# Triangular inverse of a gated delta net: 16x16 base blocks solved on GpSimd through DRAM tables in place of 8x8 blocks selected on TensorE

## The chip, the cores and the metric

The kernel runs on one core of one Trainium2 chip. The metric is device time in microseconds, as the median of several runs of the whole program. The program is one launch; all data is float32.

## What is computed

The reference is a trunk of two residual layers: a bidirectional gated delta net, a mixture of experts, multi-head latent attention, and the mixture again. Only the delta net is touched by the change. Its core, cut from the reference, for one direction:

```python
k_beta = k * beta[..., None]
a = jnp.where(strict, jnp.einsum('nbhcd,nbhsd->nbhcs', k_beta, k) * decay, 0.0)
t_inv = lax.linalg.triangular_solve(a + eye, eye, left_side=True, lower=True, unit_diagonal=True)
u = jnp.einsum('nbhcs,nbhsd->nbhcd', t_inv, v * beta[..., None])
w = jnp.einsum('nbhcs,nbhsd->nbhcd', t_inv, k_beta * jnp.exp(g)[..., None])
# then a recurrence over chunks with state S; the same on the flipped sequence; the sum is
# normalised, gated with silu(z) and multiplied by w_out
```

There are 512 tokens, model width 1024, 8 key heads of 128, and 16 value heads of 128, two for each key head. What matters here is t_inv, the inverse of a unit triangular matrix, for each chunk, each value head and each of the two directions.

## The kernel before

The function delta_net writes one block of instructions for each engine. It works in chunks of P = 128 tokens, so a sequence has TT = 4 tiles, and loops over the NK = 8 key heads. Head 0 is projected and prepared ahead of the loop; body(0, FIRST) and body(7, LAST) are written out, and a hardware loop runs body(i, MAIN) for heads 1 to 6, the middle heads. All orders are written out by hand; engines meet through semaphores.

Body i does the inverse and the recurrence of head i and, in the same time, the projections of head i + 1 and the output projection of head i - 1.

**The inverse.** mask_scores leaves A (the masked scores, for two value heads h and four tiles). compact() on VectorE picks the 8x8 diagonal blocks out of A into A8 and forms factors. Seven B steps then solve all the 8x8 blocks of both directions: in each, TensorE multiplies R8 with constant selection matrices (line 572), and VectorE multiplies and subtracts (lines 1154, 1156). VectorE spreads the blocks to 128x128 tiles of TU (line 1164), and four groups of sixteen transposes (line 582) with ScalarE copies give the turned form. Then levels l = 3 to 6 double the block each time: X = A T (make_x, line 592), masked by VectorE (line 1145), Y and V (make_y, make_v, lines 598 and 604), and updates of T and U by VectorE (line 1150). ScalarE copies the older blocks to W ahead of each level (line 803).

**What stands between.** TensorE carries a list of fillers. In FIRST and MAIN these are the 32 projection matmuls of head i + 1 (project, line 455; bank 0 or 1): eight ahead of the B steps, the rest between the steps and in the levels. In LAST they are the output projections y of head 6. VectorE's between(slot) does the convolution taps, the scans of the gate spans (line 1006), and the silu products of head i + 1 in the same manner.

**The rest of the body.** Four recurrence steps, with the gate projection z (make_z, line 541) in them; then prepare (sixteen transposes, line 510), the output projections y0 to y7 of head i - 1 (line 500) with turn_kq behind y3 (it waits for the normalised kq: squares on ScalarE, key sums on VectorE, rsqrt on GpSimd at lines 165 and 167, then normalise) and scores (line 528) behind y5; and turn_o (line 663), eight transposes.

**GpSimd** per head: the taps copies (line 909), four products qkd (line 923) once the scores are masked, two span additions (line 899), and the small rsqrt steps. **SP** issues, in a loop over n: load_w(n + 1), load_z(n), load_spans(n + 1); behind the loop the rows of the norm, and eight small transfers of the layer norm gains and biases (line 398 to tapr, semaphore cols_in; line 399 to gain_cols), then the first expert weights. In LAST, TensorE waits for cols_in behind its first three fillers.

A record in the trace is half a float32 matmul: each 128x512 matmul shows as two records, and so does each 128x128 one; a transpose shows as one.

Of the kernel before, what the change touches and what calls it, by code (L numbers as in the profile page):

```python
# [26 lines left out]
LEVELS, BASE = 7, 3  # L27
# [13 lines left out]
C_BLK = C_ROW + 8 * P  # L41
C_UNIT = C_BLK + P
C_SIDE = C_UNIT + 8
C_SEAT = C_SIDE + 16
# [6 lines left out]
def constants():  # L51
# [17 lines left out]
    for k in range(8):  # L69
        c[:, C_ROW + k * P:C_ROW + (k + 1) * P] = r == q // 8 * 8 + k  # L70
    c[:, C_BLK:C_BLK + P] = r // 8 == q // 8
    for at, value in ((C_HALF, -0.5), (C_EPS_K, 4.0 * RMS_EPS), (C_EPS_O, DH * RMS_EPS), (C_EPS_LN, LN_EPS), (C_ZERO, 0.0)):
        c[:, at:at + 8] = value
    eight = np.arange(8)[None, :]
    c[:, C_UNIT:C_UNIT + 8] = r % 8 == eight
    c[:, C_SIDE:C_SIDE + 8] = eight > r % 8
    c[:, C_SIDE + 8:C_SIDE + 16] = eight < r % 8
# [48 lines left out]
OUTPUT = [(f"y{n}", n % 2) for n in range(8)]  # L126
PREPARE_LATE = [("kT", 2), ("qT", 3), ("KK", 2), ("KQ", 3)]


def dn_uses(with_next, with_last):  # L130

    names = list(PROJECT if with_next else OUTPUT)
    names += [(f"B{m}", 4 + m % 2) for m in range(7)] + [("G0", 6), ("G1", 7), ("G2", 2), ("G3", 3)]
# [4 lines left out]
    names += [("z0", 0), ("z1", 1)]  # L138
# [5 lines left out]
    if with_next:  # L144
        names += PREPARE + OUTPUT * with_last + PREPARE_LATE + TURN_O
    else:
        names += TURN_O + [(f"end{n}", n % 2) for n in range(8)]
# [22 lines left out]
def delta_net(nc, t, dram):  # L170
# [10 lines left out]
    with ExitStack() as ctx:  # L181
# [25 lines left out]
        TU = ring[3].rearrange("p (w d h t n) -> p w d h t n", w=2, d=2, h=2, t=TT)  # L207
        bc = sb("bc", [P, 2, 2 * TT])
        A8 = sb("A8", [P, 2 * TT, 8])
        side = sb("side", [P, 2, 8, 2 * TT])  # L210
        co = sb("co", [P, 2, 8, 2 * TT])
        R8 = sb("R8", [P, 2, 2 * TT, 8])
        part8 = sb("part8", [P, 2, 2 * TT, 8])
# [13 lines left out]
        tmp = TU[:, 1, 1, 1].rearrange("p t n -> p (t n)").rearrange("p (f t g) -> p f t g", f=4, t=TT)  # L227
# [13 lines left out]
        beta_row_ready = sem("beta_row_ready")  # L241
        rows_in, R_ready, B_read, block_ready, turned_ready = (sem(n) for n in ("rows_in", "R_ready", "B_read", "block_ready", "turned_ready"))
# [18 lines left out]
        earlier = {0: 2, 1: 2, 2: 2, 3: 1, 4: 4, 5: 4, 6: 1, 7: 0}  # L261
        base = {b: n + FIRST_HEAD.per.get(b, 0) for b, n in earlier.items()}

        def read_of(name, i):
# [14 lines left out]
            if name[0] == "B":  # L279
                return B_read, i * 7 + int(name[1]) + 1  # L280
            if name[0] == "G":
                return turned_ready, i * 4 + int(name[1]) + 1
# [27 lines left out]
        def merged(which, h, l, tt=None):  # L310

            b = 1 << l
            whole = TU[:, which, 0, h]
            first, tiles = (0, TT) if tt is None else (tt, 1)
            return bass.AP(whole.tensor, whole.offset + first * P, [list(whole.ap[0]), [2 * b, tiles * P // (2 * b)], [2 * TT * P + b, 2], [1, b]])

        def row_factors(m):

            return bass.AP(co, co[:, 0, 7 - m].offset, [list(co[:, 0, 0].ap[0]), [8 + 16 * m, 2], [1, 2 * TT], [0, 8]])

        def spread(d, h):

            one = R8[:, d, h * TT]
            return bass.AP(R8, one.offset, [list(one.ap[0]), [8, TT], [0, 16], [1, 8]])

# [12 lines left out]
        def _(sp):  # L338
# [31 lines left out]

            load_w(0, False)
# [7 lines left out]
            load_z(0, False)  # L379
            load_w(1, True)  # L380
            load_rows_of_norm(sp, t, dram, 0)
# [3 lines left out]
            load_spans(1)  # L385
            sp.wait_ge(zeroed, 1)
# [30 lines left out]
        def _(pe):  # L417
# [41 lines left out]
            def log_sums():  # L459
# [9 lines left out]
                mm.then_inc(full[6], 1)  # L469

# [60 lines left out]
            def body(i, uses, with_next):  # L531
# [13 lines left out]
                if with_next:  # L545
                    for ct in range(4):
                        for a in range(KD):
                            fill.append((project, (uses, i, i + 1, ct, (a, a + 1))))
                else:
                    for n in range(8):  # L550
                        for h in range(2):
                            fill.append((project_out, (uses, "y", i, i - 1, n, h)))

                def filler(n=1):
                    for _ in range(n):
                        if fill:
                            f, a = fill.pop(0)
                            f(*a)

                filler(8 if with_next else 3)  # L560
# [4 lines left out]

                pe.wait_ge(rows_in, 16)
                for m in range(7):
                    pe.wait_ge(R_ready, i * 8 + m + 1)
                    bank = begin(uses, f"B{m}", i)
                    for d in range(2):  # L570
                        k = m if d else 7 - m
                        mm = pe.matmul(bank[:, d * 64:(d + 1) * 64], c[:, C_ROW + k * P:C_ROW + (k + 1) * P], R8[:, d].rearrange("p g j -> p (g j)"), start=True, stop=True)
                    done(mm, uses, f"B{m}")
                    filler(2 if with_next and m < 6 else 1)
                filler()
                if not with_next:
                    pe.wait_ge(weighted, 1)
                for g in range(4):
# [2168 lines left out]
```

## Time and profile before

| | |
|---|---|
| median of 3 runs | 1528.35 us (1528.23 to 1530.12) |
| span of the profiled execution | 1527.5 us |
| TensorE busy | 1457.1 us (95%), 8226 matmul records |
| TensorE weight loads | 901.5 us (59%) |
| VectorE busy | 887.9 us (58%) |
| ScalarE busy | 373.7 us (24%) |
| GpSimd busy | 169.8 us (11%) |
| mean granted TensorE clock | 0.985 |
| DMA, mean over the span | 141 GB/s |

The table counts busy time over the whole program; the delta net ends at about 850 us. TensorE's busy time contains the overlap of pipelined matmuls, so the length of a group is best read from the start of one group to the start of the next. The granted clock is a share of full speed, 1.00 or 0.50.

### The profile page before, as it was taken

The numbers are of one execution on the slowest core, as the hardware profiler recorded it, in microseconds if no ns is written. First come the engines' busy times: TensorE is split into PE (matmuls) and PEld (weight loads), VectorE is DVE, ScalarE is ACT, GpSimd is POOL, SyncE is SP. The second block draws the span as 40 slices with busy tenths as digits, with TensorE's granted clock in tenths as the row PEclk, the third lists the DMA queues.
The fourth block names the chain that finished last, engine by engine and source line by source line (L and its number), as shares of the span: only waits on it lengthen the run. The fifth ranks groups of instructions, "written<-read, shape, count | busy, mean of one in ns | idle before, by whom it ended". The sixth has DMA issues, their size and how long they took to land. (4 is left out here: it accounts for less than half of the span.)

```text
span 1527.5 us, 22499 instructions
## 1 busy us (share of the span) xinstructions
PE 1457.1 (95%) x8226; PEld 901.5 (59%) x8226; DVE 887.9 (58%) x1800; ACT 373.7 (24%) x831; POOL 169.8 (11%) x196
## 2 busy tenths in 40 slices
PE   8799999999999999999999889999999999899896
PEld 5478686685776866857769543334654454543332
DVE  2775776766857767668575545317435454734227
ACT  3223222222222222222212222110333222122210
POOL 1200203002002030020010120003100000120011
PEclk9899999999999999999999899999999999899998
DMA  7760312102121121020250469997021115489983
GB/s 223 232 210 26 99 29 83 40 15 87 39 67 52 29 82 38 17 82 0 58 191 28 151 245 399 399 362 233 0 75 44 38 39 213 158 305 400 400 327 126
DMA packets 126625, 215.50 MB, mean 141 GB/s; under 512 B 13809, under 2 KB 61233, under 8 KB 126561
## 3 DMA queue, kind: packets, MB, share of 16 engines
q1 hardware_dynamic: 112096, 169.46, 32.0%
q10 hardware_dynamic: 9536, 27.27, 4.8%
q0 software_dynamic: 4928, 17.89, 3.2%
q8 instruction: 43, 0.70, 0.2%
q14 instruction: 22, 0.17, 0.0%
HBM read 182.95 MB, written 31.65 MB: 140 GB/s over the span
## 5 line engine op out<-in xcount | busy, mean ns | idle before, releaser
L455 PE MATMUL bank<-xT,wgu 128*128 128x512 f32 x448 | 210.8, 601 | 0.0
L1798 PE MATMUL bank<-wgu,moe_xgT 128*32 128x512 f32 x1536 | 169.8, 594 | 4.4 <-issue 4.0
L500 PE MATMUL bank<-wd,oT 128*128 128x512 f32 x256 | 118.1, 604 | 2.2 <-ACT oT L849 1.3
L541 PE MATMUL bank<-wd,xT 128*128 128x256 f32 x512 | 119.8, 380 | 0.0
L455 PEld LDWEIGHTS bank<-xT,wgu 128*128 128x128 f32 x448 | 78.5, 192 | 64.4 <-issue 63.7
L1798 PEld LDWEIGHTS bank<-wgu,moe_xgT 128*32 128x32 f32 x1536 | 50.4, 110 | 105.8 <-issue 95.1
L1029 DVE SCALAR_TENSOR_TENSOR wgu<-bank,taps,wgu 128x510 f32<-128x510 f32 (+1 forms) x128 | 95.3, 745 | 12.2 <-ACT wgu L744 8.1
L541 PEld LDWEIGHTS bank<-wd,xT 128*128 128x128 f32 x512 | 95.1, 191 | 11.4
L1821 PE MATMUL bank<-wd,moe_hidT 128*32 128x512 f32 x768 | 87.1, 593 | 7.2 <-issue 4.1
L2065 DVE TENSOR_TENSOR moe_hid<-moe_silu,bank 128x256 f32<-128x256 f32 x24 | 10.1, 422 | 128.7 <-ACT moe_silu L1908 128.7
L1150 DVE TENSOR_TENSOR wgu<-wgu,bank 128x512 f32<-128x512 f32 x112 | 73.9, 683 | 9.0 <-PE bank L604 3.4
L500 PEld LDWEIGHTS bank<-wd,oT 128*128 128x128 f32 x256 | 46.9, 194 | 49.1 <-issue 49.0
L604 PE MATMUL bank<-late,wd 128*128 128x128 f32 x512 | 67.2, 277 | 0.3
L592 PEld LDWEIGHTS bank<-wgu,wd 128*128 128x128 f32 x512 | 62.0, 192 | 8.4 <-issue 7.2
L2633 DVE TENSOR_REDUCE mla_mx<-bank 128x1 f32<-128x512 f32 x32 | 22.0, 686 | 74.2 <-PE bank L2400 74.2
L1122 DVE TENSOR_TENSOR res<-res,bank 128x512 f32<-128x512 f32 x64 | 43.9, 685 | 35.3 <-PE bank L500 34.9
L592 PE MATMUL bank<-wgu,wd 128*128 128x128 f32 x512 | 64.2, 278 | 0.0
L604 PEld LDWEIGHTS bank<-late,wd 128*128 128x128 f32 x512 | 61.6, 192 | 1.7 <-DVE wd L1145 1.6
L1821 PEld LDWEIGHTS bank<-wd,moe_hidT 128*32 128x32 f32 x768 | 26.5, 110 | 60.5 <-issue 60.2
L831 ACT ACTIVATE vs<-bank,gb 128x128 f32<-128x128 f32 x96 | 30.5, 375 | 108.8 <-PE bank L641 108.8
L598 PEld LDWEIGHTS bank<-wd,late 128*128 128x128 f32 x384 | 48.6, 192 | 11.5 <-issue 11.5
L1145 DVE TENSOR_TENSOR wd<-bank,masks 128x512 f32<-128x512 f32 x64 | 44.1, 690 | 18.5 <-PE bank L592 17.4
(344 smaller groups left out, 2390.5 us busy)
## 6 DMA issues: line engine op xcount, KB each, us to landing
wgu<-moe_w_gate SPq DMA_DIRECT2D x32, 1024.0 KB, 14.2
wgu<-moe_w_up SPq DMA_DIRECT2D x32, 1024.0 KB, 15.5
wd<-moe_w_down SPq DMA_DIRECT2D x32, 1024.0 KB, 15.9
wgu<-dn_w_in SPq DMA_DIRECT2D x32, 512.0 KB, 4.0
slots_x<-gains SPq DMA_DIRECT2D x1, 9984.0 KB, 37.9
wd<-dn_w_in SPq DMA_DIRECT2D x8, 1024.0 KB, 5.5
wd<-dn_w_out ACTq DMA_DIRECT2D x16, 512.0 KB, 3.9
xT<-slots_x ACTq DMA_DIRECT2D x16, 512.0 KB, 8.5
```

Source lines behind the costliest of these rows:

```text
L455: mm = pe.matmul(bank[:], wqkv[:, ct, k], xT[:, k], start=k == 0, stop=k == KD - 1)
L500: mm = pe.matmul(ps[uses.at[f"{name}{n}"][0]][:], oT[:, h, tt], wo[:, h, half * 512:(half + 1) * 512], start=h == 0, stop=h == 1)
L541: mm = pe.matmul(bank[:, (n % 2) * 256:(n % 2) * 256 + 256], xT[:, k, tt * P:(tt + 1) * P], wz[:, k], start=k == 0, stop=k == KD - 1)
L592: mm = pe.matmul(bank[:, tt * P:(tt + 1) * P], A[:, h, tt], merged(0, h, l, tt), start=True, stop=True)
L598: mm = pe.matmul(bank[:, tt * P:(tt + 1) * P], W[:, h, tt], X[:, h, tt], start=True, stop=True)
L604: mm = pe.matmul(bank[:, tt * P:(tt + 1) * P], X[:, h, tt], W[:, h, tt], start=True, stop=True)
L1029: ins = nc.vector.scalar_tensor_tensor(out=conv[:, ct, lo:hi], in0=bank[:, lo + d:hi + d], scalar=w[:, j:j + 1], in1=conv[:, ct, lo:hi], o ...
L1122: nc.vector.tensor_tensor(y, y, bank[:], ALU.add).then_inc(y_ready, 1)
L1145: nc.vector.tensor_tensor(X[:, h], bank[:].rearrange("p (t n) -> p t n", t=TT), m, ALU.mult).then_inc(xm_ready, 1)
L1150: nc.vector.tensor_tensor(merged(which, h, l), merged(which, h, l), change, ALU.subtract).then_inc(U_ready if which else T_ready, 1)
L1798: mm = pe.matmul(ps[2][seats].rearrange("p (a f) -> p a f", a=2), xgT[:, j % ROW_BUFS, k, seats], wgu[:, e % RING, :, k], start=k == 0, st ...
L1821: mm = pe.matmul(ps[4 + half][seats], hidT[:, f, seats], wd[:, e % RING, f, half * 512:(half + 1) * 512], start=f == 0, stop=f == 1)
```

## The change

The base of the doubling goes from 8x8 to 16x16 blocks, so level 3 is gone, and the blocks are found in another way. compact(), the seven B steps, the G transposes, the spreading and their constants are removed.

SP gets solve_blocks(n): it writes A to a DRAM table A_rows (two transfers of 256 KB), waits for them, reads the diagonal blocks of 16 rows of 64 bytes into raw_blk so that each partition holds one block (four transfers, 128 partitions of 256 elements), waits for T_solved, writes the solved blocks in both forms to the diagonals of the DRAM table T_rows (two transfers of 2048 pieces of 64 bytes; off the diagonal the table was zeroed at the start), waits for T_kept, and loads the full tiles of TU back (four transfers of 512 KB, in 512-byte pieces, semaphores T_in[0] and T_in[1]).

GpSimd gets solve(i), behind qkd and ahead of the span additions of the next head: a copy of the head's betas, a scaled mask, four products S, the diagonal, 28 dependent small operations (14 columns, each a product and an addition) and two products for the two forms.

The order changes. TensorE's body begins with all 32 projection matmuls of head i + 1; then comes make_x of level 4, which waits for T_in. The fillers in the levels are now y0 to y3 of head i - 1 (all in bank 0), and only y4 to y7 remain behind the recurrence, with turn_kq behind y4 and scores behind y6. VectorE does the scans, the taps of three tiles and two silus ahead of the levels. In LAST, TensorE waits for cols_in first, then does y0 to y3 and all of z, and y4 to y7 stand in the recurrence steps. SP's order at the start and in the loop changes around solve_blocks: the large zero fill of slots_x and the rows of the norm now stand behind solve_blocks(0), and the norm rows and cols transfers at the end stand behind solve_blocks(7).

The core of the diff:

```diff
-LEVELS, BASE = 7, 3
+LEVELS, BASE = 7, 4
...
+            def solve_blocks(n):
+
+                for h in range(2):
+                    sp.wait_ge(at_ready, n * 2 + h + 1)
+                    sp.dma_start(tiles_of(t["A_rows"])[:, 4 * h:4 * h + 4], A[:, h]).then_inc(A_kept, 16)
+                sp.wait_ge(A_kept, (n + 1) * 32)
+                for h in range(2):
+                    for d in range(2):
+                        sp.dma_start(raw_blk[h * 64 + d * 32:h * 64 + d * 32 + 32], diagonal(t["A_rows"], 4 * h, 32)).then_inc(blocks_in, 16)
+                sp.wait_ge(T_solved, n + 1)
+                if head_zero(n):
+                    sp.wait_ge(padded, 16)
+                for f in range(2):
+                    sp.dma_start(diagonal(t["T_rows"][f], 0, P), T_blk[:, f]).then_inc(T_kept, 16)
+                sp.wait_ge(T_kept, (n + 1) * 32)
+                for h in range(2):
+                    for f in range(2):
+                        sp.dma_start(forms[:, f, h].rearrange("p d t n -> p (d t) n"), tiles_of(t["T_rows"][f])[:, 8 * h:8 * h + 8]).then_inc(T_in[h], 16)
...
             with sp.Fori(1, NK - 1) as n:
                 load_w(n + 1, True)
                 load_z(n, True)
                 load_spans(n + 1)
+                solve_blocks(n)
             load_z(NK - 1, True)
+            solve_blocks(NK - 1)
             sp.wait_ge(zero_filled, 32)
             load_rows_of_norm(sp, t, dram, 1)
...
                 if with_next:
                     for ct in range(4):
-                        for a in range(KD):
-                            fill.append((project, (uses, i, i + 1, ct, (a, a + 1))))
...
+                        project(uses, i, i + 1, ct)
+                if uses is not FIRST:
+                    for n in range(4 if with_next else 8):
+                        fill.append((uses, "y", i, i - 1, n))
...
                 if not with_next:
                     pe.wait_ge(cols_in, 64)
                     pe.wait_ge(*last_read(2, i))
                     pe.matmul(ps[2][:, 0:4 * KD], cols[:], ident[0:4 * KD, 0:4 * KD], start=True, stop=True).then_inc(cols_turned, 1)
...
+                    filler(4)
+                    pe.wait_ge(z_in, (i + 1) * 16)
+                    for n in range(TT):
+                        make_z(n)
                     pe.wait_ge(weighted, 1)
...
                 def make_x(l, h):
                     if l == BASE:
-                        pe.wait_ge(turned_ready, i * 4 + 2 * h + 2)
+                        pe.wait_ge(T_in[h], (i + 1) * 32)
...
+            def solve(i):
...
+                step(nc.gpsimd.tensor_tensor(scaled[:], upper, over_rows, ALU.mult))
+                pool.wait_ge(blocks_in, (i + 1) * 64)
+                for part in range(4):
+                    some = slice(32 * part, 32 * (part + 1))
+                    raw = raw_blk[some].rearrange("p r c -> p c r") if part % 2 else raw_blk[some]
+                    step(nc.gpsimd.tensor_tensor(S[some], raw, scaled[some], ALU.mult))
+                step(nc.gpsimd.tensor_tensor(S[:].rearrange("p r c -> p (r c)")[:, 0:BLK * BLK:BLK + 1], ones[:, 0:BLK], ones[:, 0:BLK], ALU.mult))
+                for k in range(BLK - 2, 0, -1):
+                    n = BLK - 1 - k
+                    part = prod[:, 0:k * n].rearrange("p (r c) -> p r c", r=k)
+                    step(nc.gpsimd.tensor_tensor(part, S[:, 0:k, k:k + 1].to_broadcast([P, k, n]), S[:, k:k + 1, k + 1:].to_broadcast([P, k, n]), ALU.mult))
+                    step(nc.gpsimd.tensor_tensor(S[:, 0:k, k + 1:], S[:, 0:k, k + 1:], part, ALU.add))
+                nc.gpsimd.tensor_tensor(T_blk[:, 1], S[:], over_cols, ALU.mult)
+                nc.gpsimd.tensor_tensor(T_blk[:, 0], S[:].rearrange("p r c -> p c r"), over_rows, ALU.mult).then_inc(T_solved, 1)
```

## Rows read from the trace of the kernel before

**Rows 1.** Windows: busy us of each engine in one middle head, clock, DMA.

```profile
360.10:453.20 93.10, 92.88 (x491) 68.96 (x490) 63.51 (x126) 24.55 (x55) 11.54 (x10) 1.00 0.14 40
```

**Rows 2.** Timeline of TensorE, same head: start us, us, line, operation, records.

```profile
345.03 1.91 PE L510 MATMUL bank<-masks,wgu 128*128 128x128 f32 x16
346.77 7.03 PE L500 MATMUL bank<-wd,oT 128*128 128x512 f32 x16
...
357.95 1.95 PE L528 MATMUL bank<-kqT 128*128 128x128 f32 x16
359.74 3.60 PE L500 MATMUL bank<-wd,oT 128*128 128x512 f32 x8
...
364.12 7.13 PE L455 MATMUL bank<-xT,wgu 128*128 128x512 f32 x16
371.09 0.55 PE L572 MATMUL bank<-R,masks 128*128 128x64 f32 x4
371.48 1.94 PE L455 MATMUL bank<-xT,wgu 128*128 128x512 f32 x4
...
386.23 2.29 PE L582 MATMUL bank<-masks,wgu 128*128 128x128 f32 x16
388.35 2.07 PE L592 MATMUL bank<-wgu,wd 128*128 128x128 f32 x16
390.26 1.88 PE L455 MATMUL bank<-xT,wgu 128*128 128x512 f32 x4
391.98 1.05 PE L598 MATMUL bank<-wd,late 128*128 128x128 f32 x8
...
395.55 1.88 PE L455 MATMUL bank<-xT,wgu 128*128 128x512 f32 x4
```

**Rows 3.** Timeline of VectorE in the same head.

```profile
359.13 1.29 DVE L1070 TENSOR_TENSOR wd<-wgu,bank 128x512 f32<-128x512 f32 x2 [0.21 <-PE bank L528]
...
391.91 1.22 DVE L1006 TENSOR_TENSOR_SCAN wgu<-wgu 128x512 f32<-128x512 f32 x1
```

**Rows 4.** Timeline of GpSimd in it; last, a group over the program (mean ns).

```profile
348.08 0.20 POOL L165 TENSOR_TENSOR kq_rs<-kq_ss,masks 128x8 f32<-128x8 f32 x1 [4.54 <-DVE kq_ss L1053]
348.36 1.64 POOL L167 TENSOR_TENSOR kq_rs<-kq_rs,masks 128x8 f32<-128x8 f32 x1
...
361.76 5.95 POOL L923 TENSOR_TENSOR wd<-wgu 128x512 f32<-128x512 f32 x4 [3.26 <-DVE wgu L1074]
...
L909 POOL COPY taps<-tap_all 128x5 f32 x12 | 7.5, 650 | 0.0
```

**Rows 5.** DMA issues by line: KB each, median us from issue to landing.

```profile
wgu<-dn_w_in SPq DMA_DIRECT2D x32, 512.0 KB, 4.0
...
wd<-dn_w_in SPq DMA_DIRECT2D x8, 1024.0 KB, 5.5
...
gate_rows<-late POOLq DMA_DIRECT2D x1, 64.0 KB, 2.1
```

**Rows 6.** DMA packets in the stretch 761.5 to 762.0.

```profile
DMA packets 1119, 0.03 MB, mean 58 GB/s; under 512 B 1100, under 2 KB 1116, under 8 KB 1119
```

**Rows 7.** The third qkd alone (min/median/max ns), and VectorE beside it.

```profile
L923 POOL TENSOR_TENSOR wd<-wgu x1: 2254/2254/2254, 364.2 to 364.2; 128x512 f32<-128x512 f32 x1
...
363.98 1.37 DVE L1083 TENSOR_TENSOR wd<-wd,masks 128x1024 f32<-128x1024 f32 x1
```

**Rows 8.** Windows ahead of the first head; the clock is the third number from the end.

```profile
56.00:59.20 3.20, 0.00 (x0) 0.00 (x0) 1.13 (x3) 0.49 (x1) 2.29 (x5) 0.50 1.07 377
59.20:65.20 6.00, 5.96 (x25) 5.49 (x26) 2.15 (x4) 1.17 (x2) 0.00 (x0) 0.50 0.85 251
```

**Rows 9.** Timeline of SP's queue ahead of the last head, first and last of ten.

```profile
754.53 0.57 SPq L1315 DMA_DIRECT2D gains<-ln_g  x1
...
759.25 0.69 SPq L398 DMA_DIRECT2D tapr<-ln_b  x1
```

More of the change, by code:

```diff
@@ L312, in merged @@
             b = 1 << l
-            whole = TU[:, which, 0, h]
+            one, other = (TU[which][dd][:, h, 0] for dd in range(2))
             first, tiles = (0, TT) if tt is None else (tt, 1)
[L315 to L324, printed above, removed]
+            return bass.AP(one.tensor, one.offset + first * P, [list(one.ap[0]), [2 * b, tiles * P // (2 * b)], [other.offset - one.offset + b, 2], [1, b]])
         def z_pair(a, n):
@@ L469, in log_sums @@
                 mm.then_inc(full[6], 1)
+                for tt in range(TT):
+                    mm = pe.transpose(ps[7][0:2 * NV, tt * P:(tt + 1) * P], gt[:, BETA, tt], ident)
+                mm.then_inc(full[7], 1)
             def turn_taps():
@@ L556, in filler @@
                         if fill:
-                            f, a = fill.pop(0)
-                            f(*a)
-                filler(8 if with_next else 3)
+                            one = fill.pop(0)
+                            for h in range(2):
+                                project_out(*one, h)
                 if not with_next:
@@ L609, in body @@
                     make_x(l, 1)
-                    filler(2 if with_next else 1)
+                    if with_next and l > BASE:
+                        filler()
                     for h in range(2):
@@ L616, in body @@
                         make_v(l, h)
-                    filler(2 if with_next else 1)
-                filler(99)
+                    if with_next and l < LEVELS - 1:
+                        filler()
                 pe.wait_ge(z_in, (i + 1) * 16)
@@ L668, in body @@
                     prepare(uses, i, i + 1)
-                    for n in range(8):
+                    for n in range(4, 8):
+                        if n == 5:
+                            turn_kq(uses, i, i + 1)
                         if uses is MAIN:
@@ L923, in body @@
                         nc.gpsimd.tensor_tensor(qkd[:, 2 * d + h], dec[:, h], kqm[:, d], ALU.mult).then_inc(qkd_ready, 1)
+                solve(i)
                 if with_next:
@@ new lines, in body @@
+                    jobs["window"] = [lambda n=n: span(i + 1, n // 2, n % 2) for n in range(4)]
+                    for ct in range(3):
+                        jobs["window"] += taps_apart(ct)
+                        if ct:
+                            jobs["window"].append(lambda ct=ct: silu(i + 1, ct - 1))
+                    for slot, job in enumerate(taps_apart(3)):
+                        jobs[slot] = [job]
+                    jobs[4] = [lambda: silu(i + 1, 2)]
+                    jobs[8] = [lambda: silu(i + 1, 3)]
```

245 lines of the change are left out of this document (106 added, 139 removed).

## The prediction

> **What bounds the kernel now.** I read the busy times of one whole head first, then TensorE in order of time, then the other engines and the queues inside the same head. In a middle head TensorE is busy 92.88 of 93.10 us at the full clock [rows 1], and in order of time its groups follow each other without a gap [rows 2]. So the delta-net heads are bound by TensorE's own work: what is removed from it comes off the time, as long as nothing it then waits for arrives later than the work that remains. The whole question is therefore how long the new road from the score matrix A to the 16x16 blocks takes, and how much TensorE work stands beside it.
>
> **What is removed from TensorE, a head.** A B step goes from 371.09 to 371.48, 0.39 us; seven are 2.7. The sixteen G transposes go from 386.23 to 388.35, 2.1. Level 3 is its X, 388.35 to 390.26, 1.9, and its Y and V, 391.98 to 395.55, 3.6 [rows 2]. Sum 10.3 us of the head, 82 us in eight. VectorE's compact(), its fourteen small operations and its level 3 go too, but it waits for TensorE today, so I price them at nothing.
>
> **The cover.** Let K be the end of the KK scores, 358.85 (half of the scores that start at 357.95 and are followed at 359.74). After the change TensorE has, behind K: KQ 0.9, y7 1.7, turn_o 1.0, and all 32 projection matmuls. Sixteen records of 512 columns take 364.12 to 371.09, 0.43 us each [rows 2]; 64 are 27.9. X of level 4 is reached at K+31.5 and X of the second value head at K+32.4. That last one needs T_in[1], the last transfer.
>
> **The new chain, from K.**
> - VectorE's masks and kqm end and GpSimd starts qkd at 361.76, K+2.9 [rows 3, 4]. A itself is ready at K+1.6; writing it (two issues, 2.1 us as for gate_rows) and reading the 64-byte rows back (four issues of 0.4, 2.1 us and 2048 packets) ends about K+9 to K+12 [rows 5, 6], beside GpSimd's own work below, so GpSimd decides.
> - qkd: three of four take 1.23 us each ((5.95 - 2.25)/3), so 4.9 [rows 4]. The four scans of VectorE, 1.22 each [rows 3], are now first in its window, right on top. The third qkd took 2.25 us in place of 1.23, while VectorE ran a product of two SBUF tensors from 363.98 [rows 7]. The scan reads two SBUF tensors as well. Bounds 0 and 4.9; I take 4.0, since the one row that overlaps lost about all of the overlap. Then beta and scaled, 1.1. K+12.9.
> - The solve: a 4 to 8 element operation costs 0.20 and the next dependent one starts 0.28 after it [rows 4]; from there to 512 elements the slope is 2.04 ns an element. Four S products of 256 elements, 3.2; the diagonal 0.3; 28 dependent steps, 28 x 0.28 + 1120 elements x 2.04 ns = 10.1; two T_blk 1.4. Sum 15.0, and 0.7 for the silu products of VectorE in the same window. K+28.6.
> - T to DRAM: 4096 packets of 64 bytes. Issue 0.8, fixed part 2.1 [rows 5]. Small packets (8 bytes nearly all) went at 1119 in 0.5 us on the 16 DMA engines, 7 ns each on one engine [rows 6]; the 512-byte ones of a projection weight at (4.0 - 2.1) us for 1024, 30 ns [rows 5]. So 1.8 to 7.7 us; no row has small writes to DRAM. I take 4.7, the middle. Together 7.6. K+36.2.
> - T back: 2.1 MB in four transfers. The z weight gives 1.05 MB in 5.5 - 2.1 us, 308 GB/s [rows 5]; 6.8 + 2.1 = 8.9. K+45.1.
> So TensorE idles 45.1 - 32.4 = 12.7 us a head, against 10.3 saved.
>
> The SBUF page of the Trainium skill ("SBUF — State Buffer", Who interferes with whom) says that a VectorE instruction with two SBUF inputs contends with a GpSimd instruction that reads SBUF, and that the loser blocks for the whole instruction; the trace agrees (2.25 against 1.23 us), and without that rule the sum would be 4.7 us shorter a head. The DMA page ("DMA: Bandwidth & Descriptors", Specifications) says that below 512 bytes a DMA reads, modifies and writes, and it speaks against the 64-byte stores; no row here shows it, and it gives no time of its own.
>
> **What else changes.** (a) TensorE's turn_kq waits for kq. Today four output projections (346.77 on) cover that chain; now only y4 does. Key sums end at 348.08, the power ends at 350.0, one VectorE product of 0.65 makes it 350.7; TensorE is there at 346.77 + 1.72 = 348.5 [rows 2, 4]. 2.3 us idle in each middle head. (b) After the idle 56.0 to 59.2 the granted clock was 0.50 for 6.0 us of work [rows 8], which is the level of 1.2 GHz in place of 2.4; it lost 3.0 us. A gap of 12.7 us should cost the same: 3.0 a head. (c) The levels have half the filler, but VectorE and ScalarE have one level and all small steps less beside them; nothing, and 1 for the first head, which has no filler. (d) spans, z weights and the next projection weights stand in SP's queue around solve_blocks. The spans and z are issued before it, the weights of n+2 after T_kept, a whole level stage before they are needed; nothing. (e) The zero fill moves behind head 0's solve and has 40 us of slack; nothing. (f) four BETA transposes and beta's rows at the start: 1 us.
>
> **The last head.** SP issues the norm rows and the cols transfers only behind solve_blocks(7), which waits for T_kept. But in the last body TensorE waits for cols_in before its first filler. So the y and z work that is meant to cover the solve starts only when cols is in. There the scans are missing: T_kept at 45.1 - 8.9 - 4.7 = K+31.5. Four T_in issues 1.6, then norm and cols issues, 754.53 to 759.94 = 5.4 [rows 9], K+38.5; T_in and norm rows are 3.1 MB in the same rings, 10.2 us from K+31.9, so cols lands at K+44.2. TensorE waits from K+3.6: 40.6 us. Less 10.3, plus 3.0 clock, plus 2 for recurrence steps in which y (1.7 us) stands in for z (16 records of 256 columns, 3.5): +35.3.
>
> **Sum.** Six middle heads: -10.3 + 12.7 + 2.3 + 3.0 = +7.7 each, +46. First head: its cover lacks y7 and turn_o (2.7), but its kq wait is there today: -10.3 + 15.4 + 3.0 = +8.1, with 1 for missing fillers +9. Last +35, start +1. Together +91 on a span of 1527.5: 1618.5, and 0.85 us lie between this span and the median: 1619. With no lock and 7 ns packets the chain is 37.5, the idle 5.1: +0.1 x 6 + 2 + 32 + 1 = +36, 1564. With 30 ns packets and the lock in full, 3.9 more in each of eight heads: 1650.
>
> The Trainium skill ("GPSIMD Engine Reference", Performance pitfalls) has reads with a step of over 8 bytes 50% dearer; no row here shows it, and it would add 1.2 us a head.
>
> **Rivals.** (1) The road is cheap: small packets near 7 ns, no lock that matters. 1564, still slower, because the last head's wait and the kq wait stay. For it: the 7 ns row. Against: those are loads. 0.18. (2) The cover holds and it is faster: the chain is under 32.4 us from K, 12.7 less than my sum, so that the 10.3 come off whole. Place: T_in[1] in the middle heads; it decides from K+32.4. Middle -8.0 x 6, first -10, last 35 - 13 = +22, start +1: -35, 1493. For it: each fixed part of 2.1 us may overlap with its issue and GpSimd's real spacing may be under its recorded spans. Against: GpSimd's steps alone end at K+24 without any lock, and two round trips of 2.1 us and 2.1 MB follow. 0.13. (3) GpSimd's small strided operations in the loop cost more: the taps copy of 5 elements took 0.65 us there [rows 4], 0.45 more than the step I price; 28 x 0.45 = 12.6 in eight heads, +101: 1720. Against: the rsqrt add, just as small, took 0.20. 0.14. (4) The change does not do what it says, the solve not being on the road at all: excluded by make_x's wait for T_in.
>
> **How the numbers follow.** Forecast as summed 0.55 (its own range 1564 to 1650), rivals 0.18, 0.13, 0.14. Range 1540 to 1700: it leaves out rival 2 and about half of rival 3. About 0.2% is what a measurement can tell from no change; only a mix of rival 1 and 2 lands there. Faster 0.13, same 0.02, slower 0.85.
>
> **What would show it.** Right: TensorE idle before line make_x at level 4 of some 13 us in each middle head, released by the DMA of T_rows; granted clock 0.5 behind it; an idle stretch of about 40 us in the last head ahead of the cols matmul; idle of 2 us ahead of the kq transposes; the third and fourth qkd or the scans stretched. Wrong: T_in landing before the projections end, dependent GpSimd steps spaced far from 0.28 us, T_rows writes landing in under 5 or over 11 us, or cols_in before the solve is written.

## The result and the profile of the changed kernel

The changed kernel takes 1593.12 us as the median of four runs (1592.22 to 1599.55), against 1528.66 us for the kernel before in the same session. The ratio is 1.0427, 95% interval 1.0406 to 1.0447: slower by 4.3%. The forecast was 1619 us with a range of 1540 to 1700, so its sign and its range held and its middle was 26 us too high. The profiled execution spans 1591.1 us, 63.6 more than that of before, at a mean granted clock of 0.942 (0.985 before).

The busy times on the page of the changed kernel, then a group of section 5 (busy us, mean ns of one | idle ahead of them and what ended it):

```profile
PE 1402.6 (88%) x7494; PEld 846.8 (53%) x7494; DVE 796.8 (50%) x1569; ACT 346.5 (22%) x767; POOL 296.0 (19%) x497
...
L595 PE MATMUL bank<-wgu,wd 128*128 128x128 f32 x384 | 62.1, 323 | 62.6 <-DMA wgu<-T_rows 62.6
```

TensorE has 54.5 us less busy time and still ends 63.6 us later: it stands idle. The waits of TensorE in the delta net's heads (us in total, times, longest) say for whom:

```profile
PE bank L595 <- DMA wgu<-T_rows: 62.6, 14, 10.1
PE bank L581 <- DMA tapr<-ln_b: 38.9, 1, 38.9
PE bank L538 <- DVE kq L1108: 19.2, 7, 4.2
```

L595 is make_x at level 4, which waits for the solved tiles; L581 is the cols matmul of the last head; L538 is turn_kq. Here is one middle head in order of time on TensorE. It is the part that answers to [rows 2]; K, the end of the KK scores, is 479.63.

```profile
474.21 1.25 PE L538 MATMUL bank<-masks,kq 128*128 128x128 f32 x8 [2.50 <-DVE kq L1108]
...
478.73 1.95 PE L547 MATMUL bank<-kqT 128*128 128x128 f32 x16
...
483.64 27.73 PE L471 MATMUL bank<-xT,wgu 128*128 128x512 f32 x64 [0.37 <-DVE res L1152]
518.01 2.07 PE L595 MATMUL bank<-wgu,wd 128*128 128x128 f32 x8 [6.64 <-DMA wgu<-T_rows]
521.62 2.07 PE L595 MATMUL bank<-wgu,wd 128*128 128x128 f32 x8 [1.54 <-DMA wgu<-T_rows]
523.49 1.92 PE L601 MATMUL bank<-wd,late 128*128 128x128 f32 x8
```

The projections end at K+31.7, and the two value heads of X start at K+38.4 and K+42.0. What happened on GpSimd in the same time (answering to [rows 4]):

```profile
482.54 7.70 POOL L957 TENSOR_TENSOR wd<-wgu 128x512 f32<-128x512 f32 x4 [7.46 <-DVE wgu L1120]
490.19 1.13 POOL L928 COPY beta_n<-beta_blk 128x16 f32 x1
491.40 0.73 POOL L934 TENSOR_TENSOR scaled<-masks,beta_n 128x256 f32<-128x256 f32 x1
492.29 3.35 POOL L939 TENSOR_TENSOR S<-raw_blk,scaled 32x256 f32<-32x256 f32 x4 [0.16 <-POOL scaled L934]
496.02 0.21 POOL L944 TENSOR_TENSOR prod<-S 128x14 f32<-128x14 f32 x1
...
505.97 0.62 POOL L946 TENSOR_TENSOR T_blk<-S,beta_n 128x256 f32<-128x256 f32 x1
506.55 0.84 POOL L947 TENSOR_TENSOR T_blk<-S,beta_n 128x256 f32<-128x256 f32 x1
```

On VectorE, the four scans lie on top of the qkd products, and SP issues the transfers (the length is that of the issues; answering to [rows 5]):

```profile
483.51 7.82 DVE L1052 TENSOR_TENSOR_SCAN wgu<-wgu 128x512 f32<-128x512 f32 x4
```

```profile
480.63 0.97 SPq L368 DMA_DIRECT2D A_rows<-wd  x2
483.85 1.92 SPq L372 DMA_DIRECT2D raw_blk<-A_rows  x4
507.41 1.38 SPq L377 DMA_DIRECT2D T_rows<-T_blk  x2
511.95 3.88 SPq L381 DMA_DIRECT2D wgu<-T_rows  x4
```

So the chain of one middle head, from K: qkd starts at 2.9 and takes 7.7; beta and scaled; S starts at 12.7; the 28 steps take 9.95 (496.02 to 505.97); both forms are done at 27.8; the store is issued and has landed, with its two issues, 4.5 us later (507.41 to 511.95); the loads bring the last tile at 42.0, 9.7 us on.

How fast the DMA engines moved the two kinds of pieces that the kernel stores, first A in pieces of 512 bytes, then T in pieces of 64 (the last two numbers are the DMA share and GB/s):

```profile
481.60:483.40 1.80, 1.67 (x10) 0.94 (x8) 1.80 (x4) 0.00 (x0) 0.86 (x1) 1.00 0.99 283
508.50:511.40 2.90, 2.88 (x7) 0.95 (x5) 0.66 (x1) 0.00 (x0) 1.78 (x2) 1.00 0.82 87
```

The granted clock behind the idle stretch (columns as in [rows 1]):

```profile
516.00:518.00 2.00, 0.00 (x0) 0.00 (x0) 0.00 (x0) 0.09 (x1) 0.00 (x0) 0.50 1.21 290
522.00:524.00 2.00, 2.00 (x11) 2.00 (x11) 0.20 (x1) 0.14 (x1) 0.00 (x0) 0.50 1.22 290
526.00:530.00 4.00, 4.00 (x25) 3.37 (x24) 2.95 (x6) 0.77 (x2) 0.00 (x0) 0.86 0.02 6
```

0.50 is the level of 1.2 GHz in place of 2.4: eight records of X take 2.07 us here, and sixteen took 2.07 before [rows 2].

The last head, on TensorE and on SP. Its cols matmul is reached right behind turn_o and waits 38.9 us; the issue it waits for is the last line, behind the store, the loads and the norm rows.

```profile
799.69 1.04 PE L670 MATMUL bank<-masks,late 128*128 128x128 f32 x8
839.62 0.63 PE L581 MATMUL bank<-masks,tapr 32*128 32x32 f32 x2 [38.89 <-DMA tapr<-ln_b]
840.18 9.29 PE L519 MATMUL bank<-wd,oT 128*128 128x512 f32 x16
```

```profile
821.12 1.34 SPq L377 DMA_DIRECT2D T_rows<-T_blk  x2
825.64 3.99 SPq L381 DMA_DIRECT2D wgu<-T_rows  x4
829.67 1.74 SPq L1331 DMA_DIRECT2D gains<-ln_g  x1
...
834.67 0.41 SPq L414 DMA_DIRECT2D tapr<-ln_b  x1
```

**Where the 63.6 us lie**, by the starts of the same TensorE work in both traces. From the scores of head 0 to turn_o behind head 0: 97.4 us before, 101.1 after, +3.7. Six middle heads, from turn_o to turn_o: 612.3 before, 637.4 after, +25.0 or 4.2 each. The last, from turn_o to the beta product behind the delta net (L680, now L687): 71.9 before, 102.6 after, +30.7. Everything behind that: 684.7 before, 688.8 after, +4.1. The start is 0.1 later.

A middle head adds up: -10.3 of removed work, +8.2 idle for the solved tiles, +2.5 for kq, +0.4 ahead of the projections (VectorE's addition of y), and the half clock: 0.9 on X of the first value head (2.07 against 1.16 at the full clock) and 2.6 from the second X on (the experiment e6 gives that), together +4.3.

### The profile page after: what moved, and what is told of

It reads as the page before. It is cut to its first block and busy times, and to the rows that moved or that the text cites. A ratio compares the mean times of both kernels' runs of the same rounds, so it can differ in the third digit from the quotient of the medians.

```text
span 1591.1 us, 21047 instructions
## 1 busy us (share of the span) xinstructions
PE 1402.6 (88%) x7494; PEld 846.8 (53%) x7494; DVE 796.8 (50%) x1569; ACT 346.5 (22%) x767; POOL 296.0 (19%) x497
## 5 line engine op out<-in xcount | busy, mean ns | idle before, releaser
L471 PE MATMUL bank<-xT,wgu 128*128 128x512 f32 x448 | 193.9, 593 | 1.9 <-DVE res L1152 1.9
L471 PEld LDWEIGHTS bank<-xT,wgu 128*128 128x128 f32 x448 | 84.6, 190 | 106.8 <-issue 103.7
L519 PE MATMUL bank<-wd,oT 128*128 128x512 f32 x256 | 123.1, 614 | 1.0 <-issue 1.0
L595 PE MATMUL bank<-wgu,wd 128*128 128x128 f32 x384 | 62.1, 323 | 62.6 <-DMA wgu<-T_rows 62.6
L595 PEld LDWEIGHTS bank<-wgu,wd 128*128 128x128 f32 x384 | 57.7, 232 | 76.1 <-issue 63.4
L1175 DVE TENSOR_TENSOR wd<-bank,masks 128x512 f32<-128x512 f32 x48 | 33.0, 689 | 102.1 <-PE bank L595 102.1
L2081 DVE TENSOR_TENSOR moe_hid<-moe_silu,bank 128x256 f32<-128x256 f32 x24 | 10.1, 421 | 131.8 <-ACT moe_silu L1924 131.8
L957 POOL TENSOR_TENSOR wd<-wgu 128x512 f32<-128x512 f32 x32 | 58.7, 1863 | 58.0 <-DVE wgu L1120 58.0
L813 ACT COPY late<-wgu 128x512 f32<-128x512 f32 x48 | 29.6, 618 | 165.2 <-DVE wgu L1180 101.8
L1180 DVE TENSOR_TENSOR wgu<-wgu,bank 128x512 f32<-128x512 f32 x80 | 54.5, 688 | 19.6 <-PE bank L607 13.3
L1463 POOL DMA_INDIRECT wgu<-slots_y,fetch x8 | 8.6, 1080 | 281.0 <-DMA slots_y<-moe_y_rows 268.6
L1052 DVE TENSOR_TENSOR_SCAN wgu<-wgu 128x512 f32<-128x512 f32 x32 | 58.6, 1886 | 4.6 <-DMA wgu<-gate_rows 4.6
## 6 DMA issues: line engine op xcount, KB each, us to landing
wd<-moe_w_down SPq DMA_DIRECT2D x32, 1024.0 KB, 15.7
```

Source lines behind the costliest of these rows:

```text
L471: mm = pe.matmul(bank[:], wqkv[:, ct, k], xT[:, k], start=k == 0, stop=k == KD - 1)
L519: mm = pe.matmul(ps[uses.at[f"{name}{n}"][0]][:], oT[:, h, tt], wo[:, h, half * 512:(half + 1) * 512], start=h == 0, stop=h == 1)
L595: mm = pe.matmul(bank[:, tt * P:(tt + 1) * P], A[:, h, tt], merged(0, h, l, tt), start=True, stop=True)
L957: nc.gpsimd.tensor_tensor(qkd[:, 2 * d + h], dec[:, h], kqm[:, d], ALU.mult).then_inc(qkd_ready, 1)
L1052: nc.vector.tensor_tensor_scan(row, row, mask, 0.0, ALU.add, ALU.mult).then_inc(span_ready, 1)
L1175: nc.vector.tensor_tensor(X[:, h], bank[:].rearrange("p (t n) -> p t n", t=TT), m, ALU.mult).then_inc(xm_ready, 1)
```

## The experiments

Each kernel is the changed one with one edit, unless said otherwise; the ratio is always to the kernel before, and the differences in us are between profiled spans, from 1591.1. The executions of one kernel lie 2.6 to 9.5 us apart, and the profiled one is the fastest of its kernel in e1, e5 and e6 and the slowest in e2 and e3, so a difference of spans is good to some 4 us; by the medians the savings are 23.7 (e1), 19.0 (e2), 33.1 (e3), 19.1 (e5), 8.5 (e6) and 19.6 (e7). What is read inside a head does not have this spread.

**e1: the gain columns ahead of the solve on SP.** This isolates the last head.

```diff
             load_z(NK - 1, True)
+            for j, (name, layer) in enumerate((("ln1_g", 0), ...)):    # cols and gain_cols
+                ...
             solve_blocks(NK - 1)
-            ...
```

> Change of the changed kernel: SP issues the cols and gain transfers of the last head ahead of solve_blocks(7) instead of behind it; all else is as in it. Theory (the last head pays for the order of SP's queue): the wait of 38.9 us for cols is gone, the y and z work runs while GpSimd solves, and TensorE then meets T_in after 25 us where it lands after some 38: about 28 us less, 1565 us, with a T_in wait of 10 to 12 us in the last head. Rival (that wait only stands in for the chain of the solve, which ends as late): 1590 or more.

Measured: median 1569.42, ratio 1.0254 (1.0214 to 1.0294), span 1563.3, 27.8 less. TensorE no longer stands ahead of the cols matmul; the work that was meant as cover now covers, and what is left is a wait for the tiles:

```profile
800.44 0.40 PE L581 MATMUL bank<-masks,tapr 32*128 32x32 f32 x2
802.23 7.11 PE L519 MATMUL bank<-wd,oT 128*128 128x512 f32 x16 [1.38 <-ACT oT L851]
```

The wait for the tiles in this head, next in line, is 8.4 us. From turn_o to the beta product the last head takes 76.2 us (799.48 to 875.71) in place of 102.6. So 26.4 of the 63.6 us are a matter of the order in one queue, not of the solve itself.

**e2: the four scans of VectorE behind the taps of three tiles,** so that they no longer run beside qkd.

```diff
-                    jobs["window"] = [lambda n=n: span(i + 1, n // 2, n % 2) for n in range(4)]
+                    jobs["window"] = []
                     for ct in range(3):
                         ...
+                    jobs["window"] += [lambda n=n: span(i + 1, n // 2, n % 2) for n in range(4)]
```

> Change of the changed kernel: VectorE's four scans stand behind the taps of the first three tiles instead of ahead of them, so that they run when GpSimd has ended its solve. Theory (GpSimd and two-SBUF-input VectorE work shut each other out): qkd goes from 7.7 to about 5.0 us a head, the scans from 2.2 to 1.2 us each, T_in lands 2.7 to 3.6 us earlier in seven heads, 1568 to 1574 us. Rival (GpSimd's products are as slow by themselves there): qkd stays at 7.7, 1593 us.

Measured: median 1574.08, ratio 1.0281 (1.0260 to 1.0301), span 1573.7, 17.4 less. The wait for T_rows is 42.5 us in place of 62.6. On GpSimd the four qkd products and the beta copy are short again:

```profile
473.43 4.96 POOL L957 TENSOR_TENSOR wd<-wgu 128x512 f32<-128x512 f32 x4 [7.46 <-DVE wgu L1120]
478.32 0.21 POOL L928 COPY beta_n<-beta_blk 128x16 f32 x1
```

4.96 against 7.70 and 0.21 against 1.13: the overlap with the scans costs the chain 3.7 us a head; here both forms of T are done at K+24.3 in place of K+27.8. The first middle head gains nothing, since its blocks land only at K+13.2. The scans pay as well: 7.82 us for four beside qkd, 1.22 each alone [rows 3]. The two groups together lasted 8.8 us (482.54 to 491.33), and one after the other they would last 9.8; running them side by side gains little. Single records of the changed kernel show how:

```profile
485.92 2.18 POOL L957 TENSOR_TENSOR wd<-wgu 128x512 f32<-128x512 f32 x1
486.96 2.22 DVE L1052 TENSOR_TENSOR_SCAN wgu<-wgu 128x512 f32<-128x512 f32 x1
```

The first product takes 1.28 us and the first scan 1.39; the other three of each take 2.2. They end in turn, product and scan, at 483.82, 484.90, 485.96, 487.04, 488.10, 489.18, 490.25 and 491.33, 1.1 us apart, and the beta copy of 16 elements ends together with the last scan (490.19 + 1.13 = 491.32). So a record of 2.2 us is one turn of waiting and one of work. This bears out for the scan too the rule that the prediction cites from the Trainium skill ("SBUF — State Buffer", Who interferes with whom), that the one that loses waits for the whole instruction of the other.

**e3: half of the columns of the solve.** Seven of the fourteen columns, so fourteen small operations, are left out; the inverse is then incomplete, so this time is only a dose of the chain's length.

```diff
-                for k in range(BLK - 2, 0, -1):
+                for k in range(BLK - 2, 7, -1):
```

> Change of the changed kernel: the solve does only the first 7 of its 14 column steps (the other seven are left out of the computation), 14 dependent small GpSimd operations less. Theory (GpSimd's string of small operations is on the road in every head): 14 x 0.35 = 5.0 us less wait in each of eight heads, 1553 us, somewhat less if the clock no longer falls. Rival (the transfers or the SP queue set the end): under 10 us less, 1585 or more.

Measured: median 1560.07, ratio 1.0182 (1.0151 to 1.0213), span 1559.6, 31.5 less. The wait for T_rows is 32.0 us, 30.6 less, or 4.4 in each of the seven heads that have it; that for cols is 34.1, 4.8 less, so cols does stand behind GpSimd's solve. Together 35.4 us of waits are gone and 31.5 came off the span; 1.7 of the difference lies behind the delta net. A middle head tells more: the second X starts 5.0 us earlier (K+37.0 in place of K+42.0 in the same head), and the head is only 3.6 us shorter (102.3 in place of 105.9). Behind the wait of 2.50 us for kq the two output projections take 5.2 to 5.3 us in all six middle heads, in place of 3.60; the granted clock is 0.64 from 559 to 563 us, behind such a wait. Doing half of the columns takes off half of what the change costs, so it would not pay for the change.

**e4 and e6: spare matmuls that keep TensorE at work in the gap,** to price the clock. They write a bank whose next real matmul starts it anew. e4 puts seven ahead of X of the first value head; e6 puts three more ahead of the second.

```diff
                 def make_x(l, h):
+                    if l == BASE and with_next:
+                        spare = begin(uses, f"X{l}{h}", i)
+                        for k in range((7, 3)[h]):
+                            pe.matmul(spare[:], xT[:, 0, 0:P], xT[:, k], start=True, stop=True)
                     if l == BASE:
```

> Change of the changed kernel: seven spare 512-column matmuls (6.0 us) into the bank of X stand ahead of the wait for T_in in every body but the last; their result is overwritten. Theory (the idle lets the granted clock fall and the work behind it pays): the clock stays at 1.00 around level 4, X, Y and V run at full rate, 3.3 us less in seven heads, 1570 us; the time of T_in's landing doesn't move. Rival (level 4 is slow because it waits for masks and copies): 1593 us or more.

Measured for e4: median 1596.46, ratio 1.0425 (1.0405 to 1.0445), span 1594.6, 3.5 more. The expectation failed. The first gap was filled and X of the first value head ran at the full clock (1.16 us), but a second idle stretch of 2.54 us follows it, and the clock fell there:

```profile
519.55 1.16 PE L599 MATMUL bank<-wgu,wd 128*128 128x128 f32 x8 [0.71 <-DMA wgu<-T_rows]
523.24 2.07 PE L599 MATMUL bank<-wgu,wd 128*128 128x128 f32 x8 [2.54 <-DMA wgu<-T_rows]
```

In one of the six middle heads the clock stayed at full speed behind the same idle of 2.53 us, and in four of them it fell later, behind the wait of 2.50 us for kq. So e4 did not separate anything, and e6 was made for it.

> Change of the changed kernel: spare matmuls ahead of both waits for T_in, seven ahead of X of the first value head and three between it and X of the second. The run with seven alone moved the idle behind the first X, where the clock then fell at 522 us all the same. Theory (the clock's fall costs 3.3 us a head): with no idle stretch of over 2 us left the clock stays at 1.00 through level 4, 18 to 23 us less than the changed kernel, 1572 us. Rival (it costs nothing that the wait would not cost): 1593 us.

Measured for e6: median 1584.63, ratio 1.0352 (1.0335 to 1.0369), span 1581.5, 9.6 less, half of what I expected. In the five later middle heads X and what follows run at the full clock (X takes 1.16 us); one of them:

```profile
515.71 1.16 PE L599 MATMUL bank<-wgu,wd 128*128 128x128 f32 x8 [0.62 <-DMA wgu<-T_rows]
...
519.32 1.16 PE L599 MATMUL bank<-wgu,wd 128*128 128x128 f32 x8
...
523.89 1.88 PE L519 MATMUL bank<-wd,oT 128*128 128x512 f32 x4
```

X of the second value head starts 42.89 us behind the start of the scores (476.43), just as in the changed kernel (478.73 to 521.62). From there to the first filler it is 4.57 us here, 7.18 there (521.62 to 528.80). So the half clock costs 2.6 us behind the second X; the 0.9 on the first X lies inside the wait for the second and gives nothing back. Over six heads that is 15.7, and in the span 9.6 came. In the first head level 4 ends at 111.94 against 112.35, so next to nothing came there. The trace shows where the rest went. In the first middle head a wait of 3.9 us is left, the clock falls behind it, and the six spare records take 4.4 us, so that the second X starts 2.2 us later than in the changed kernel. And in three of the six middle heads, that one among them, the clock falls later on, behind the wait for kq:

```profile
470.21 1.25 PE L538 MATMUL bank<-masks,kq 128*128 128x128 f32 x8 [2.50 <-DVE kq L1112]
471.30 5.30 PE L519 MATMUL bank<-wd,oT 128*128 128x512 f32 x8
```

5.2 to 5.3 us in place of 3.60; in the changed kernel this happens in the first middle head alone, and in part (4.66). From the scores of the first middle head to those of the last head e6 is 8.7 us shorter, which is most of the 9.6.

**e5: solve ahead of qkd on GpSimd.** VectorE's scans then meet the solve's wait for the blocks.

```diff
+                solve(i)
                 pool.wait_ge(dec_ready, i * 2 + 2)
                 pool.wait_ge(mask_ready, i * 2 + 2)
                 ...                                  # the four qkd products
-                solve(i)
```

> Change of the changed kernel: GpSimd does solve(i) ahead of its four qkd products instead of behind them. Theory (qkd stands on the road ahead of the solve, and the blocks land 2.7 us before GpSimd is free): T_in lands 2.7 us earlier in seven heads, nothing in the last one, 1574 us; the scans run beside an idle GpSimd at 1.2 us. Rival (the block reads land no earlier than GpSimd is free today): 1590 us or more.

Measured: median 1574.07, ratio 1.0278 (1.0261 to 1.0295), span 1568.9, 22.2 less; the wait for T_rows is 40.1. The four qkd products stood on the chain although the first to need them is the recurrence (L659). What is next late is the road of A: S now waits for raw_blk and starts at K+9.2, against K+12.7 in the changed kernel (K is 467.74 here).

```profile
476.95 3.35 POOL L939 TENSOR_TENSOR S<-raw_blk,scaled 32x256 f32<-32x256 f32 x4 [12.82 <-DMA raw_blk<-A_rows]
```

The first middle head gains less, since its blocks land only at K+11.6.

**e7: turn_kq and scores behind y5,** that is two output projections ahead of turn_kq in place of one, and y6 and y7 behind the scores.

```diff
-                        if n == 5:
+                        if n == 6:
                             turn_kq(uses, i, i + 1)
+                            scores(uses, i, i + 1)
                         if uses is MAIN:
                             ...                      # y
-                        if n == 6:
-                            scores(uses, i, i + 1)
```

> Change of the changed kernel: TensorE does y4, y5, then turn_kq and scores at once, then y6 and y7, in place of y4, turn_kq, y5, y6, scores, y7. Theory (the kq wait of 2.5 us a head lacks cover, and work behind the scores is cover for the solve): the kq wait falls to some 0.6 and 0.8 us appear at the scores, and 1.7 us more stand behind them: 2.8 us less in each of six heads, 1576 us. Rival (the wait moves to the scores, whose ScalarE copies have no cover now): 1590 us or more.

Measured: median 1573.49, ratio 1.0280 (1.0263 to 1.0297), span 1571.4, 19.7 less. The wait for kq is 12.3 us in place of 19.2, that for T_rows 57.7 in place of 62.6, and the 0.4 ahead of the projections is gone. y6 now stands behind K and widens the cover. The blocks land later, at K+10.3 in the head at 468.84 in place of K+9.1, which qkd still hides in this kernel.

**e8: e1, e5 and e7 together, with two spare matmuls ahead of each of the two waits** in the heads that have a next one.

> Change of the changed kernel: the cols transfers ahead of solve_blocks(7), qkd behind the solve, the order y4, y5, turn_kq, scores, y6, y7, and two spare matmuls ahead of each wait for T_in (but in the last head). Theory (four costs, each of which adds): 28 for the last head, 2.7 and 1.7 us of wait, 1.1 of the kq wait and 3 of the clock in the others: 1508 us, faster than the kernel before. Rival (the parts share one wait, and taking one away leaves the others to fill it): 1540 us or more.

Measured: median 1516.26, ratio 0.9908 (0.9892 to 0.9925), span 1513.8. This version is 0.9% faster than the kernel before and 5% faster than the changed one (0.9908 / 1.0427 = 0.950), though 8 us over what I expected of it. A middle head of it (in the first two of the six the clock still falls at the first X):

```profile
452.64 1.25 PE L538 MATMUL bank<-masks,kq 128*128 128x128 f32 x8 [0.78 <-DVE kq L1111]
454.06 2.02 PE L547 MATMUL bank<-kqT 128*128 128x128 f32 x16 [0.17 <-ACT kqT L794]
...
490.95 1.16 PE L599 MATMUL bank<-wgu,wd 128*128 128x128 f32 x8 [1.20 <-DMA wgu<-T_rows]
491.94 1.88 PE L592 MATMUL bank<-xT 128*128 128x512 f32 x4
494.56 1.16 PE L599 MATMUL bank<-wgu,wd 128*128 128x128 f32 x8 [0.74 <-DMA wgu<-T_rows]
...
499.13 1.88 PE L519 MATMUL bank<-wd,oT 128*128 128x512 f32 x4
```

and the start of S on GpSimd, which now waits for the blocks:

```profile
465.31 3.35 POOL L942 TENSOR_TENSOR S<-raw_blk,scaled 32x256 f32<-32x256 f32 x4 [10.85 <-DMA raw_blk<-A_rows]
```

That is K+10.4. Here two of the edits meet: the order of e7 makes the blocks land later, and with the solve ahead of qkd nothing hides it any more. Against e5 they land 1.1 to 1.7 us later in five middle heads and 2.5 in the first of the six, 9 us in all, which is about what this version fell short by.

**e9: e8 without the spare matmuls,** for what they alone are worth.

> Gain columns ahead of the solve on SP, solve ahead of qkd on GpSimd, kq turned and scored behind y5, as in e8_all, but without the spare matmuls ahead of the two waits for the solved tiles. It tells what those spare matmuls are worth. Theory (an idle of about 3 us is enough to bring the granted clock to half, which then costs some 2 us or more of each middle head): idle ahead of X is 1.2 + 1.9 = 3.1 us in the first place and 1.5 us in the second in each middle head, the clock is at half behind it, and the kernel is slower than e8_all by 6 x 1.5 to 6 x 2.5, so 1525 to 1531 us. Rival (the clock stays up over idles this short, and the spare work only fills time that is waited anyway): within 3 us of e8_all, 1513 to 1519 us.

Measured: median 1528.50, ratio 0.9980 (0.9971 to 0.9990), span 1526.0, 12.2 more than e8. The three edits alone gave 27.8, 22.2 and 19.7, 69.7 in all, and together 65.1 (by the medians 62.4 and 64.6): within what a span can tell, they add up. The same head:

```profile
456.94 2.02 PE L547 MATMUL bank<-kqT 128*128 128x128 f32 x16 [0.17 <-ACT kqT L790]
...
494.00 2.07 PE L595 MATMUL bank<-wgu,wd 128*128 128x128 f32 x8 [3.10 <-DMA wgu<-T_rows]
497.61 2.07 PE L595 MATMUL bank<-wgu,wd 128*128 128x128 f32 x8 [1.54 <-DMA wgu<-T_rows]
...
503.62 1.88 PE L519 MATMUL bank<-wd,oT 128*128 128x512 f32 x4
```

The tiles are no earlier with the spare work: the second X starts 40.5 us behind the scores in e8 and 40.7 in e9. From it to the first filler it is 4.57 us in e8 and 6.01 in e9, which makes 1.6 us of this head (45.07 against 46.68 from the scores to the first filler). The first head gives another 1.6 (level 4 ends at 105.45 against 107.00). The first middle head is the exception: it is 1.9 us longer with the spare work. From the first scores to those of the last head the spare work saves 9.6 of the 12.2 us; 3.5 lie behind the delta net, in code that is the same in both, and the last head takes 0.7 back. The rival, that the clock stays up over idles this short, falls.

A table of tiles laid out with longer rows, so that the load back would run in larger pieces, was not tried.

## Why the prediction was right, and what was off

**The mechanism held at each of its three places.** TensorE idles ahead of make_x at level 4, released by the DMA of T_rows, with the clock at 0.50 behind it; it idles ahead of the cols matmul in the last head; and it idles 2.5 us ahead of turn_kq, where 2.3 were foretold. e1, e5 and e2, and e7 each take away the cause of one and get its time back. The removed 10.3 us a head are borne out by the sum of a middle head, which closes with them to 0.1 us, and e9, with three orders mended and nothing else, comes out at 0.998 of the kernel before.

**The cover** was to be K+31.5 and was K+31.7. **GpSimd's part** was to end at K+28.6 and ended at K+27.8. In it the lock was priced at 4.0 and cost 2.7 on qkd, and another 0.9 on the beta copy, which I had not seen: that the sum is so near is in part luck. The 28 steps took 9.95 against 10.1, and the silu products, priced at 0.7 besides, are in the 9.95 (one step took 0.70 in place of 0.29); rival 3, the dear small operation, did not occur in the solve. The beta copy of 16 elements shows what such a row was: 1.13 us beside the scans, 0.21 without.

**The step that was mis-sized is "T to DRAM".** I took 7.6 us: 0.8 of issue and a fixed part of 2.1, and behind them 4.7 for packets, the middle between 7 and 30 ns a packet. It took 4.5. Two things were off. The packets ran for 3.1 us (508.37 to 511.44), at 87 GB/s in the window above. That is 12 ns a packet on each of 16 engines, between the two rows and nearer to that of 7. And issue and fixed part leave only 1.4 us outside the packets, not 2.9, since the packets of the first transfer already ran while the second was being issued (507.83 to 508.79). So small stores did have a price: the pieces of 512 bytes of A went to DRAM at 283 GB/s, about 30 ns a packet, so a piece of 64 bytes carries an eighth of the data and costs two fifths of the time. The rule that the prediction cites from the Trainium skill ("DMA: Bandwidth & Descriptors", Specifications), that below 512 bytes a DMA reads, modifies and writes, gives no time; the trace agrees that such stores fall below the rate of larger ones, and no run shows whether the engine reads first. **T back** was to take 8.9 and took 9.7: 290 GB/s in the windows above, where I took 308 from the z weight [rows 5], which explains 0.4 of the 0.8. Together the chain is K+42.0 in place of K+45.1, and the idle 8.2 in place of 12.7; the last 1.4 of that difference is mostly the first X, which ran at half clock inside the wait (2.07 in place of 1.16).

**The sum, term by term.** A middle head +4.2 against +7.7: 21 us of the error of 27 (63.6 against 91). Its idle was 4.5 us smaller, the clock cost 3.5 where I had 3.0, and kq and the addition of y gave 0.6 more. The first head +3.7 against +9, 5 us: it waited 11.6 (10.1 and 1.5) against 15.4, for the same reason; the other 1.5 I cannot place. The last head +30.7 against +35: the cols wait was 38.9 against 40.6, and the clock behind it cost 2.2 (the y of 16 records take 9.29 there and 7.11 in e1) against 3.0; recurrence steps with y in place of z cost less than the 2 I gave them. Behind the 38.9 two errors nearly cancel, which is luck: T was in DRAM at K+28.6, not 31.5, and the four load issues took 4.0 us, not 1.6. Start 0.1 against 1. Against all this stands +4.1 behind the delta net, where I had nothing; without it the forecast would have been 4 us further off. These terms give 63.6 in place of 91.

**What stays open** is why that +4.1. The trace shows where most of it lies, in the first mixture of experts, and both times it is the granted clock: in the routing, 0.50 from 940.5 to 944.5 where the kernel before has 0.98 (881 to 884), 2.2 us; and behind an idle of 2.04 us that stands in both traces, 0.72 from 1047 to 1053 where the kernel before has 1.00, 1.7 us. In the nine kernels of the experiments the same stretch takes 685 to 691 us, with 684.7 before, and its code is the same in all of them. No run shows why the clock falls there in one and not in the other.

**A slip of mine:** I called the stretch 360.10 to 453.20 [rows 1] one whole middle head. A head takes 102 us (612.3 / 6); the stretch is 91% of one. What I read from it, that TensorE has no gap, holds, and the 93.1 enters no term.

**The rivals.** Rival 1 (cheap small packets, no lock that matters; 1564) was right in one half and only in part: the packets took 3.1 us, where it has 1.8 and the sum 4.7, and the lock cost 3.7. Rival 2 (the cover holds; 1493) needed the chain under K+32.4, and it was K+42.0; in the middle heads of e8 the second X still starts at K+39.6 or later. The error of 26 us lay toward rival 1; of the 3.1 us by which I priced the store too high, 1.6 are the packets' and 1.5 are issue and fixed time that I had not let run beside them.

## What to carry to other kernels

Before counting what is taken off the busiest engine, write the whole replacing chain, with both trips through DRAM, against the work that is left to cover it. Then look at what stands ahead of and beside each of its links in the same queue: the transfer that a later wait needs behind the solve on SP, products that nobody needs yet ahead of it on GpSimd, scans on VectorE that slow it. Here mending the order in three places (SP, GpSimd, TensorE), and leaving the solve as it was, turned +4.3% into -0.2%, or -0.9% with TensorE kept at work in the last gap.

## What the runs showed of the hardware

- 4096 pieces of 64 bytes were stored to DRAM in 4.5 us, two issues included; the packets moved at 87 GB/s, where stores in pieces of 512 bytes moved at 283.
- Two idle stretches of 3.10 and 1.54 us were enough for half the granted clock (e9), and 2.54 us behind 1.2 us of work too (e4); stretches of 1.20 and 0.74 with X and 1.9 us of spare work between them left it at 1.00 (e8).
- The same idle does not always do the same. Behind the wait of 2.50 us for kq the two output projections took 3.60 us in five of the six middle heads of the changed kernel, 5.2 to 5.3 in all six of e3 and in three of the six of e6. A short wait can cost 1.7 us of slow work behind it, and what is saved ahead of it can be lost there.
- A VectorE scan and a GpSimd product, both of 128x512, take 1.22 and 1.24 us alone. Side by side they take turns of 1.1 us, and each record lasts 2.2.
- A dependent chain of 28 small GpSimd operations (14 to 56 elements) advances 0.36 us an operation, of which 0.21 to 0.30 are the operation itself.
- A product of 256 elements that reads its source turned took 0.84 us against 0.62, 35% more, though its other operand is spread another way too; in the four products S, where only the turned source differs, it is 0.84 against 0.72, 17%. The 50% that the prediction cites from the Trainium skill ("GPSIMD Engine Reference", Performance pitfalls for Q7 kernels) is more than these rows have.
